# Diagonal and finest-level attention scores as channel sums of elementwise products, in the heads of a hybrid decoder step

## The chip, the cores and the metric

The kernel runs on one core of a Trainium2 chip. The metric is the device time of one execution in microseconds (us). Engines: TensorE (matmuls; PE in the profile, its weight loads PEld), VectorE (DVE), ScalarE (ACT), GpSimd (POOL) and SyncE (SP), which issues most of the transfers. They run side by side and meet at semaphores.

## The reference

One layer of a decoder for 256 prompt tokens and 8 sample tokens: a norm, a wide input projection, two gated recurrences (HGRN2 with 8 heads of 128 keys and 128 values, GLA with 4 heads of 128 keys and 256 values), their merge, an output projection, a squared-ReLU MLP and gated embeddings, all in float32. What matters here is the recurrence of the prompt, per head:

```python
b = jnp.cumsum(gi, axis=-2)
diff = b[..., :, None, :] - b[..., None, :, :]
decay = jnp.exp(jnp.where(causal, diff, -jnp.inf))
scores = jnp.einsum('bhtk,bhsk,bhtsk->bhts', qi, ki, decay)
o = jnp.einsum('bhts,bhsv->bhtv', scores, vi) + ...
```

The score of a token t with an earlier token s is a sum over 128 channels of q, k and a decay that depends on channel, t and s. With s = t the decay is 1 and the score is the sum of q times k over the channels.

## The kernel before

**The stream.** All weights come as tiles of 128 output rows, each in two slabs of 128 x 1024. For each slab SP loads `raw`, ScalarE rounds it to `whi` (L355, `round_slab`), VectorE takes the rest `wlo` (L360, `rest_slab`), and TensorE multiplies: three products of 264 columns for each of 8 blocks (L380 to L382). Rounded operands have the type fp32r; a sum of three such products stands in for a float32 product. Four slots (`RING`) hold slabs; SP loads a slot again when VectorE has taken its rest, ScalarE rounds into it again when TensorE has multiplied it.

**The heads.** After the projections come twelve heads (H = 0 to 7 HGRN, 8 to 11 GLA), each beside four weight tiles, that is eight slabs of TensorE. Each engine has its program for a head written out by hand: `slab(k)` calls, and between them the head's own work. TensorE's slab(k) is slab k of the head's tiles; ScalarE's and VectorE's slab(k) is the one that TensorE multiplies two slabs later, so their slab(6) to slab(9) belong to the next head's first slabs or the last of this one. Every engine does its list in order.

**A head's scores.** The prompt is taken as two blocks of 128 tokens, the second one in mirrored order. Level 0 pairs the two blocks; level l = 1 to 7 pairs the halves of cells of 2h tokens, h = 128 >> l, so the finest, level 7, has h = 1. For each level, decay factors for q and k are made in `lev` (VectorE subtracts, ScalarE takes the exponential in `decays`), and multiplied with q and k by VectorE in `level_operands` (L1540 to L1544). The q side stays in `lev[:, l, 0, :]`, the k side goes to `k_lev`. TensorE then does, in `scores`, two diagonal products of k_b and q_b (L766), seven products for levels 1 to 7 (L768) and one for level 0 (L770), each 128 x 128 x 128 in float32, that is unrounded, which the profile lists as two records. VectorE masks the level scores with `both` (L1581), the diagonal blocks and level 0 with `ident` (L1584), and adds the levels into `pairs` (L1592). Then `prob_v` (L787, L788) multiplies `pairs` with the values.

**The order around it.** TensorE in a head: slabs 0 to 4, `turn_v` (transposes of the values, L757), `scores`, `turn_kd` (transposes of kd, L778), slabs 5 and 6, `prob_v`, `state` (in HGRN heads), slab 7 with the norm's sums inside. `scores` waits for VectorE's level products, `turn_kd` for VectorE's kd (L1559) and for ScalarE's copy of the turned values, `v_tok` (L1096), which shares a bank with it. ScalarE: slabs 2 to 6, `turned` (the v_tok copy), slab 7, the copy of kd, the squares for the norm and, in HGRN heads, their rounding `sq_hi` (L1153), slab 8, logs and exponentials, slab 9, `decays` of the next head, `b_hi`. VectorE: slab 2, level products, slab 3, level products, kd, slabs 4 and 5, a tile's drain, slab 6, masks and adds, slab 7, the next head's level factors, `sq_lo` (L1603) in HGRN heads, slab 8, more factors, slab 9, the output. In HGRN heads the norm is already done with `ones_r` and two rounded operands, `sq_hi` and `sq_lo` (L801, L802). GpSimd copies `cum`, `q_b` and `k_b` of the next head (L1934 to L1939) and in GLA heads adds the two squares (L1944).

Of the kernel before, what the change touches and what calls it, by code (L numbers as in the profile page):

```python
# [28 lines left out]
P = 128  # L29
D_MODEL = 2048  # L30
KT = D_MODEL // P
NP_TOK = 256
# [69 lines left out]
def build(nc, t):  # L102
# [79 lines left out]
    with nc.sbuf_tensor("gate_w", [2 * RANK, GH * P], F32) as gate_w, nc.sbuf_tensor("rank_z", [2 * RANK, TOK], F32) as rank_z:  # L182
        pass
    S = sb("S", [P, 2, UNIT])
    n_states = [S[:, 0, :], S[:, 1, :], samp[:, 0:UNIT]]
# [5 lines left out]
    with nc.sbuf_tensor("o_first", [P, TOK], F32), nc.sbuf_tensor("sq_lo", [P, NP_TOK], F32R) as sq_lo:  # L191
# [57 lines left out]
    by_engine = {  # L249
        "act": ["v_tok_ready", "lev_exp", "kd_exp", "kd_tok_ready", "sq_ready", "sq_rounded",  # L250
                "ln_rs", "rs_ready", "o_hi_done", "s_out_ready", "sg_abs", "sg_exp", "sg_ln", "sg_sigma"],
        "dve": ["sq_parted", "lev_sub", "lev_ready", "kd_ready", "masked", "probs_ready", "sg_ls",
                "sg_ready", "o_scaled", "o_gated", "o_done"],
# [51 lines left out]
    def before(H):  # L305

        return H + 1

    def cells(ap, h, at, step, pitch):

        return bass.AP(ap.tensor, ap.offset + at, [list(ap.ap[0]), [step, 2], [pitch, 64 // h], [1, h]])
# [4 lines left out]
    def lefts(ap, h):  # L316
        return cells(ap, h, 0, P + h, 2 * h)

    def packed(ap, h):
# [144 lines left out]
    def _(sp):  # L464
# [17 lines left out]
        for k in range(RING, KT - 4):  # L482
            load_wide(sp, T_RANK, k, T_RANK)
            if k in (RING, RING + 3):
                load_x(4 + (k - RING) // 3)
        for dst, name in ((masks, "masks"), (ident, "ident"), (head_gain, "head_gain"),
                          (gate_b, "gate_b")):
            sp.dma_start(dst[:], t[name]).then_inc(const_landed, 16)
        for part in range(2):
            sp.dma_start(gate_w[part * RANK:(part + 1) * RANK, :], t["gate_w"]).then_inc(const_landed, 16)  # L490
# [181 lines left out]
    def _(pe):  # L672
# [27 lines left out]
        pe.wait_ge(tiles_drained, T_RANK + WIDE)  # L700
        pe.wait_ge(const_landed, 16 * 6)
        for h in range(GH):
# [58 lines left out]
        def scores(H, D):  # L761
            pe.wait_ge(h_sem["lev_ready"], now(H))
            pe.wait_ge(h_sem["ln_rs"], before(H))
            for B in range(2):
                at = slice(B * P, (B + 1) * P)
                pe.matmul(DG[:, 2 * B * P:(2 * B + 1) * P], k_b[:, at], q_b[:, at], start=True, stop=True)  # L766
            for l in range(1, LEVELS):
                pe.matmul(SC[(l - 1) // 4][:, (l - 1) % 4 * P:((l - 1) % 4 + 1) * P], k_lev[:, l - 1, :], lev[:, l, 0, :],  # L768
                          start=True, stop=True)
            pe.matmul(DG[:, P:2 * P], lev[:, 0, 1, :], lev[:, 0, 0, :], start=True, stop=True)\  # L770
              .then_inc(h_sem["scores_done"], 1)

# [8 lines left out]
        def prob_v(H, D):  # L781

            pe.wait_ge(h_sem["probs_ready"], now(H))
            pe.wait_ge(h_sem["o_scaled"], before(H))
            for d in range(D):
                v = slice(d * P, (d + 1) * P)
                pe.matmul(O[d][:, 0:2 * P], v_tok[:, 0, v], pairs[:, 0:2, :], start=True, stop=False, skip_group_check=True)  # L787
                mm = pe.matmul(O[d][:, P:2 * P], v_tok[:, 1, v], pairs[:, 2, :], start=False, stop=True, skip_group_check=True)  # L788
            mm.then_inc(h_sem["pv_done"], 1)
# [8 lines left out]
        def head_norm(H, D):  # L798
            if D == 1:
                pe.wait_ge(h_sem["sq_parted"], now(H))  # L800
                pe.matmul(DG[:, 0:NP_TOK], ones_r[:], sq_hi[:], start=True, stop=False)  # L801
                pe.matmul(DG[:, 0:NP_TOK], ones_r[:], sq_lo[:], start=False, stop=True).then_inc(h_sem["ss_done"], 1)  # L802
                return
            pe.wait_ge(h_sem["sq_added"], now(H - HH))
            pe.matmul(DG[:, 0:NP_TOK], ones[:], sq[:, 0, 0:NP_TOK], start=True, stop=True).then_inc(h_sem["ss_done"], 1)

        def head(H, D, first=False):
            T = 4 * H + T_HEADS

            def slab(k, midway=None, at=HT // 2):  # L810
                j, half = k // 2, k % 2
                par = (T_HEADS + j) % 2
# [124 lines left out]
    def _(act):  # L937
# [178 lines left out]
        def head(H, D, next_D, first=False):  # L1116
# [34 lines left out]
            if D == 1:  # L1151
                act.wait_ge(h_sem["sq_ready"], now(H))
                act.copy(sq_hi[:], sq[:, 0, 0:NP_TOK]).then_inc(h_sem["sq_rounded"], 1)  # L1153
            if first:
# [172 lines left out]
    def _(dve):  # L1327
# [158 lines left out]
        dve.wait_ge(gates_stored, GH)  # L1486
        dve.wait_ge(const_landed, 16 * 6)
        dve.wait_ge(masks_ready, 1)
# [26 lines left out]
        def head(H, D, more=True, opening=False):  # L1515
# [20 lines left out]
            def level_operands(l):  # L1536
# [5 lines left out]
                lq, lk = packed(lev[:, l, 0, :], h), packed(lev[:, l, 1, :], h)  # L1542
                dve.tensor_tensor(lq, lq, rights(q_b[:], h), ALU.mult)
                return dve.tensor_tensor(cells(k_lev[:, l - 1, :], h, 0, h, 2 * h), lk, lefts(k_b[:], h), ALU.mult)  # L1544

            def first_levels():

                dve.wait_ge(h_sem["kq_ready"], now(H))
                dve.wait_ge(h_sem["lev_exp"], now(H))
# [3 lines left out]
            def last_levels():  # L1553
# [30 lines left out]
            dve.tensor_tensor(pairs[:], DG[:, 0:3 * P].rearrange("s (b t) -> s b t", b=3),  # L1584
                              ident[:].rearrange("s (b t) -> s b t", b=3), ALU.mult).then_inc(h_sem["masked"], 1)
            for l in range(1, LEVELS):
                h = HALF[l]
                to = cells(pairs[:, 0, :], h, h, 2 * P - h, 2 * h)
                of = packed(probs[:, l - 1, :], h)

                dve.wait_ge(h_sem["masked"], (LEVELS + 1) * H + (l + 3))
# [9 lines left out]
            if D == 1:  # L1601
                dve.wait_ge(h_sem["sq_rounded"], now(H))
                dve.tensor_tensor(sq_lo[:], sq[:, 0, 0:NP_TOK], sq_hi[:].bitcast(F32), ALU.subtract).then_inc(h_sem["sq_parted"], 1)  # L1603
            slab(8)
# [266 lines left out]
    def _(pool):  # L1871
# [27 lines left out]

        pool.wait_ge(const_landed, 16 * 6)  # L1900

# [29 lines left out]
        def head(H, D):  # L1931
# [7 lines left out]
            pool.tensor_copy(k_b[:, 0:NP_TOK], k).then_inc(h_sem["kq_ready"], 1)  # L1939

        def add_halves(H):

# [5 lines left out]
        for i, (hg, gla) in enumerate(((hk, zk), (hk, zk))):  # L1948
# [4 lines left out]
            else:  # L1953
                pool.tensor_copy(to[:, 0:HH, :], hg[:, :, at])
                pool.tensor_copy(to[:, HH:HEADS, :], gla[:, :, at])
        pool.tensor_copy(by_head(s_cols[:, 3, :, :]), gates[:, :, at]).then_inc(cols_ready, 1)
        with pool.Fori(1, HH) as H:
            head(H, 1)
        with pool.Fori(HH, HH + 1) as H:
            head(H, 2)  # L1960
        with pool.Fori(HH, HEADS - 1) as H:
            head(H + 1, 2)
            add_halves(H)
        add_halves(HEADS - 1)
# [98 lines left out]
```

## Time and profile before

| | |
|---|---|
| median of three runs | 1628.49 us (1628.38 to 1629.86) |
| the profiled execution's own time | 1628.97 us |
| its span, first to last instruction | 1627.2 us |
| granted TensorE clock | 1.00 (2.4 GHz) |
| TensorE busy | 1620.3 us (100%) |
| VectorE, ScalarE, GpSimd busy | 1109.9, 842.2, 181.7 us |
| HBM read, written | 310.08 MB, 18.30 MB |

A busy matmul engine is listed with overlapping records: a matmul's row is longer than the distance to the next one's start, and it is the distance that the engine is held. The same holds, less so, for VectorE and ScalarE, whose next instruction starts before the row of the last one ends. The chain that ended last gives each step the time that it adds.

### The profile page before, as it was taken

Reading aid. Unit: us, or ns where it says so; the run is one execution under the profiler, and the core shown is the slowest. Engines: PE = TensorE matmul, PEld = TensorE weight load, DVE = VectorE, ACT = ScalarE, POOL = GpSimd, SP = SyncE. Lnnn points to the kernel's source line nnn. Section 1 sums busy time; section 2 is a strip of 40 time slices with the busy share of each in tenths; the row PEclk is TensorE's granted clock in tenths of the full one; section 3 lists DMA queues with packets and bytes.
Section 4 is the critical chain, followed back from the end, with each engine's and each line's share of the span. In section 5 each row is a group of like instructions: output and inputs, shape, how many; then the busy total and the mean of one; then the engine's idle time right before and its main releaser. Section 6 shows DMA issues by size and latency. Waiting matters only on the chain.

```text
span 1627.2 us, 35049 instructions
## 1 busy us (share of the span) xinstructions
PE 1620.3 (100%) x13332; PEld 1615.8 (99%) x13332; DVE 1109.9 (68%) x1917; ACT 842.2 (52%) x1192; POOL 181.7 (11%) x166
## 2 busy tenths in 40 slices
PE   9999999999999999999999999999999999999999
PEld 9999999999999999999999999999999999999999
DVE  7548767888888876655986665566555665555774
ACT  7575765666666665433654334443444334443452
POOL 3101000111111100055300000000000000035200
PEclk9999999999999999999999999999999999999999
DMA  9577895565555467755675865588557775555564
GB/s 274 161 230 225 267 270 174 164 191 162 192 166 181 155 206 229 270 181 185 173 214 186 247 207 180 188 259 243 174 181 242 245 222 185 181 197 181 167 192 144
DMA packets 151178, 329.17 MB, mean 202 GB/s; under 512 B 16944, under 2 KB 79536, under 8 KB 150608
## 3 DMA queue, kind: packets, MB, share of 16 engines
q1 hardware_dynamic: 143888, 326.00, 64.3%
q10 hardware_dynamic: 7232, 2.43, 0.6%
q8 instruction: 33, 0.54, 0.1%
q14 instruction: 25, 0.20, 0.0%
HBM read 310.08 MB, written 18.30 MB: 202 GB/s over the span
## 4 chain that ended last, share of the span: by engine, by line
PE 98%; DMA 1%; DVE 1%; ACT 0%; SPq 0%; issue 0%
PE bank L380 29%; PE bank L381 29%; PE bank L382 28%; PE bank L398 3%; PE bank L400 3%; PE bank L403 2%; PE bank L768 1%; DMA raw<-in_stream 1%; PE bank L795 0%; PE bank L787 0%; PE bank L766 0%; PE bank L788 0%; PE bank L757 0%; PE bank L732 0%; PE bank L770 0%; PE bank L778 0%
## 5 line engine op out<-in xcount | busy, mean ns | idle before, releaser
L355 ACT CAST whi<-raw 128x1024 fp32r<-128x1024 f32 x532 | 547.9, 1048 | 470.7 <-PE bank L382 388.5
L380 PE MATMUL bank<-a_hi,whi 128*128 128x264 f32 x2576 | 734.2, 285 | 0.1
L381 PE MATMUL bank<-a_hi,wlo 128*128 128x264 f32 x2576 | 729.7, 283 | 0.0
L382 PE MATMUL bank<-a_lo,whi 128*128 128x264 f32 x2576 | 729.4, 283 | 0.0
L360 DVE TENSOR_TENSOR wlo<-raw,whi 128x1024 fp32r<-128x1024 f32 x518 | 629.6, 1246 | 109.8 <-ACT whi L355 108.8
L380 PEld LDWEIGHTS bank<-a_hi,whi 128*128 128x128 f32 x2576 | 485.2, 188 | 0.8 <-issue 0.7
L381 PEld LDWEIGHTS bank<-a_hi,wlo 128*128 128x128 f32 x2576 | 485.5, 188 | 0.1
L382 PEld LDWEIGHTS bank<-a_lo,whi 128*128 128x128 f32 x2576 | 482.9, 187 | 0.0
L380 PE MATMUL bank<-b_hi,whi 128*128 128x264 f32 x1280 | 363.1, 284 | 0.0
L381 PE MATMUL bank<-b_hi,wlo 128*128 128x264 f32 x1280 | 362.6, 283 | 0.0
L382 PE MATMUL bank<-b_lo,whi 128*128 128x264 f32 x1280 | 362.4, 283 | 0.0
L381 PEld LDWEIGHTS bank<-b_hi,wlo 128*128 128x128 f32 x1280 | 241.2, 188 | 0.0
L380 PEld LDWEIGHTS bank<-b_hi,whi 128*128 128x128 f32 x1280 | 241.1, 188 | 0.0
L382 PEld LDWEIGHTS bank<-b_lo,whi 128*128 128x128 f32 x1280 | 239.9, 187 | 0.0
L1281 ACT ACTIVATE lev<-lev 128x264 f32<-128x264 f32 x64 | 27.2, 425 | 165.5 <-DVE lev L1777 165.5
L1690 DVE TENSOR_TENSOR room<-room,bank 128x264 f32<-128x264 f32 (+1 forms) x48 | 20.6, 429 | 106.9 <-PE bank L382 106.9
L1883 POOL TENSOR_TENSOR sq<-room 128x264 f32<-128x264 f32 x2 | 2.2, 1086 | 721.9 <-DVE room L1690 620.0
L398 PE MATMUL bank<-b_hi,whi 128*128 128x264 f32 x256 | 73.3, 286 | 0.3 <-DVE b_lo L1339 0.3
L403 PE MATMUL bank<-b_hi,wlo 128*128 128x264 f32 x256 | 72.8, 284 | 0.0
L400 PE MATMUL bank<-b_lo,whi 128*128 128x264 f32 x256 | 72.7, 284 | 0.0
L1783 DVE TENSOR_TENSOR a_lo<-lev,a_hi 128x264 f32 (+1 forms) x64 | 27.3, 432 | 63.8 <-ACT a_hi L1283 63.8
L1777 DVE SCALAR_TENSOR_TENSOR lev<-bank,r_bc 128x264 f32<-128x264 f32 x64 | 27.1, 432 | 52.6 <-PE bank L382 52.5
(222 smaller groups left out, 1497.7 us busy)
## 6 DMA issues: line engine op xcount, KB each, us to landing
raw<-in_stream SPq DMA_DIRECT2D x532, 512.0 KB, 4.7
m_spill<-stage SPq DMA_DIRECT2D x32, 132.0 KB, 3.7
lev<-m_spill SPq DMA_DIRECT2D x16, 264.0 KB, 2.8
room<-in_x SPq DMA_DIRECT2D x7, 528.0 KB, 7.8
S<-in_state_hgrn SPq DMA_DIRECT2D x6, 512.0 KB, 6.7
out_new_hgrn_sample<-S SPq DMA_DIRECT2D x6, 512.0 KB, 6.8
S<-in_state_gla SPq DMA_DIRECT2D x5, 512.0 KB, 6.7
out_new_gla_sample<-S SPq DMA_DIRECT2D x5, 512.0 KB, 7.5
```

Source lines behind the costliest of these rows:

```text
L355: act.copy(whi[:, s, :], raw[:, s, :]).then_inc(hi_ready, 1)
L360: dve.tensor_tensor(wlo[:, s, :], raw[:, s, :], whi[:, s, :].bitcast(F32), ALU.subtract).then_inc(lo_ready, 1)
L380: pe.matmul(out, whi[:, s, w], hi[:, k0 + k, :], start=start and k == 0, stop=False)
L381: pe.matmul(out, wlo[:, s, w], hi[:, k0 + k, :], start=False, stop=False)
L382: mm = pe.matmul(out, whi[:, s, w], lo[:, k0 + k, :], start=False, stop=stop and k == HT - 1)
L398: pe.matmul(out, whi[:, s, w], hi[:, k, :], start=k == 0, stop=False, skip_group_check=True)
L400: mm = pe.matmul(out, whi[:, s, w], lo[:, k, :], start=False, stop=rank and k == KT - 1, skip_group_check=True)
L403: return pe.matmul(out, wlo[:, s, w], hi[:, k, :], start=False, stop=k == KT - 1, skip_group_check=True)
L1281: act.activation(u, u, ACT.Square).then_inc(u_ready, 1)
L1690: ins = dve.tensor_tensor(out, out, MM[par][:, 0:TOK], ALU.add)
L1777: dve.scalar_tensor_tensor(out=u, in0=bank[:, 0:TOK], scalar=0.0, in1=r_bc[:], op0=ALU.max, op1=ALU.mult).then_inc(tiles_drained, 1)
L1783: dve.tensor_tensor(a_lo[:, T - T0, :], u, a_hi[:, T - T0, :].bitcast(F32), ALU.subtract).then_inc(a_lo_ready, 1)
```

## The change

In every head, the two diagonal products and the level 7 product leave TensorE. Their scores are needed only where s = t, or between the two tokens of a pair, so each is one number per token: a sum over the channels (partitions) of an elementwise product. GpSimd multiplies q_b and k_b into two thirds of a new buffer `dots` (`dots_of`), VectorE multiplies the two sides of level 7 into the other third. ScalarE rounds the 384 columns to `dots_hi`, VectorE takes the rest `dots_lo`, and TensorE multiplies `ones_r` with both into 384 columns of the bank DG (`sum_dots`), after `turn_kd`. VectorE then masks level 7 from DG in an instruction of its own. The order of the blocks in `pairs` and `ident` changes, for which `ident` is loaded in three parts. VectorE's slab(6) moves from before the masks to behind the adds. The semaphores `sq_rounded` and `sq_parted` become `parts_rounded` and `parts_ready`, counted twice in an HGRN head. GpSimd's first `dots_of` waits until the sample states are summed, since `dots` lies where they lay.

```diff
     def scores(H, D):
-        pe.wait_ge(h_sem["lev_ready"], now(H))
+        pe.wait_ge(h_sem["lev_ready"], first_now(H))
         pe.wait_ge(h_sem["ln_rs"], before(H))
-        for B in range(2):
-            at = slice(B * P, (B + 1) * P)
-            pe.matmul(DG[:, 2 * B * P:(2 * B + 1) * P], k_b[:, at], q_b[:, at], start=True, stop=True)
-        for l in range(1, LEVELS):
+        for l in range(1, LEVELS - 1):
             pe.matmul(SC[(l - 1) // 4][...], k_lev[:, l - 1, :], lev[:, l, 0, :],
                       start=True, stop=True)
-        pe.matmul(DG[:, P:2 * P], lev[:, 0, 1, :], lev[:, 0, 0, :], start=True, stop=True)\
-          .then_inc(h_sem["scores_done"], 1)
+        pe.matmul(DG[:, 3 * P:4 * P], lev[:, 0, 1, :], lev[:, 0, 0, :], start=True, stop=True)
+
+    def sum_dots(H, D):
+        pe.wait_ge(h_sem["parts_ready"], dots_now(H, D))
+        pe.matmul(DG[:, 0:3 * P], ones_r[:], dots_hi[:], start=True, stop=False)
+        pe.matmul(DG[:, 0:3 * P], ones_r[:], dots_lo[:], start=False, stop=True).then_inc(h_sem["scores_done"], 1)
...
         scores(H, D)
         turn_kd(H)
+        sum_dots(H, D)
         slab(5)
...
 # ScalarE, head
         slab(5)
+        act.wait_ge(h_sem["kq_ready"], second_now(H))
+        act.wait_ge(h_sem["lev_ready"], second_now(H))
+        act.copy(dots_hi[:], dots[:]).then_inc(h_sem["parts_rounded"], 1)
         slab(6)
         turned(H, D)
...
 # VectorE, level_operands
+            if l == LEVELS - 1:
+                return dve.tensor_tensor(lk, lk, lefts(k_b[:], h), ALU.mult)
 # VectorE, last_levels, behind the kd product
+            dve.wait_ge(h_sem["lev_ready"], first_now(H))
+            dve.tensor_tensor(dots[:, 0:P], lev[:, LEVELS - 1, 0, :], lev[:, LEVELS - 1, 1, :], ALU.mult).then_inc(h_sem["lev_ready"], 1)
 # VectorE, head
         slab(4)
+        dve.wait_ge(h_sem["parts_rounded"], dots_now(H, D))
+        dve.tensor_tensor(dots_lo[:], dots[:], dots_hi[:].bitcast(F32), ALU.subtract).then_inc(h_sem["parts_ready"], 1)
         slab(5)
         ...
-        slab(6)
         dve.wait_ge(h_sem["scores_done"], now(H))
         dve.wait_ge(h_sem["pv_done"], before(H))
-        for n, (first, last) in enumerate(((0, 4), (4, LEVELS - 1))):
+        for n, (first, last) in enumerate(((0, 4), (4, LEVELS - 2))):
             ...
-        dve.tensor_tensor(pairs[:], DG[:, 0:3 * P]..., ident[:]..., ALU.mult)
+        dve.tensor_tensor(probs[:, LEVELS - 2, :], DG[:, 0:P], both[:, LEVELS - 2, :], ALU.mult).then_inc(h_sem["masked"], 1)
+        dve.tensor_tensor(pairs[:], DG[:, P:4 * P]..., ident[:]..., ALU.mult)
         for l in range(1, LEVELS):
             ...
+        slab(6)
...
 # GpSimd
+    def dots_of(H):
+        pool.wait_ge(h_sem["kq_ready"], first_now(H))
+        pool.tensor_tensor(turned_blocks(dots), q_b[:, 0:NP_TOK]..., k_b[:, 0:NP_TOK]..., ALU.mult).then_inc(h_sem["kq_ready"], 1)
...
+    pool.wait_ge(units_summed, HEADS)
+    with pool.Fori(0, 1) as H:
+        dots_of(H)
     with pool.Fori(1, HH) as H:
         head(H, 1)
+        dots_of(H)
...
 # SyncE
-        for dst, name in ((masks, "masks"), (ident, "ident"), (head_gain, "head_gain"),
-                          (gate_b, "gate_b")):
+        for dst, name in ((masks, "masks"), (head_gain, "head_gain"), (gate_b, "gate_b")):
             sp.dma_start(dst[:], t[name]).then_inc(const_landed, 16)
+        for to, of in ((0, 0), (1, 2), (2, 1)):
+            sp.dma_start(ident[:, to * P:(to + 1) * P], t["ident"][:, of * P:(of + 1) * P]).then_inc(const_landed, 16)
```

## Rows read from the trace of the kernel before

**Rows 1.** The page's busy times and chain, and the heads' window (busy us, records).
```profile
PE 1620.3 (100%) x13332; PEld 1615.8 (99%) x13332; DVE 1109.9 (68%) x1917; ACT 842.2 (52%) x1192; POOL 181.7 (11%) x166
...
PE 98%; DMA 1%; DVE 1%; ACT 0%; SPq 0%; issue 0%
...
264.50:587.00 322.50, 322.39 (x2650) 320.21 (x2649) 272.62 (x708) 200.83 (x291) 44.58 (x46) 1.00 0.54 172
```

**Rows 2.** The chain in heads 1, 4, 8 and 9: start, us added, step, records.
```profile
295.56 0.69 PE bank L766 x4
...
377.88 1.56 PE bank L768 x14
...
486.48 0.45 PE bank L766 x4
...
515.18 0.56 PE bank L766 x4
```

**Rows 3.** Timeline of TensorE at head 4's norm: start, length, line, form.
```profile
388.79 0.28 PE L801 MATMUL bank<-sq_hi,ones_r 128*128 128x256 f32 x1
388.90 0.28 PE L802 MATMUL bank<-sq_lo,ones_r 128*128 128x256 f32 x1
```

**Rows 4.** Timeline of VectorE in head 4, idle time before in brackets.
```profile
376.43 0.28 DVE L1544 TENSOR_TENSOR k_lev<-lev,k_b 128x128 f32<-128x128 f32 x1
376.63 0.42 DVE L1559 TENSOR_TENSOR kd<-kd,k_b 128x256 f32<-128x256 f32 x1
376.97 2.35 DVE L360 TENSOR_TENSOR wlo<-raw,whi 128x1024 fp32r<-128x1024 f32 x2
379.24 0.42 DVE L1373 TENSOR_TENSOR stage<-bank,r_bc 128x264 f32<-128x264 f32 x1
...
382.36 2.25 DVE L1592 TENSOR_TENSOR pairs<-pairs,probs 128x128 f32<-128x128 f32 x7
...
387.61 0.42 DVE L1603 TENSOR_TENSOR sq_lo<-sq,sq_hi 128x256 fp32r<-128x256 f32 x1
...
393.50 1.23 DVE L360 TENSOR_TENSOR wlo<-raw,whi 128x1024 fp32r<-128x1024 f32 x1 [1.45 <-ACT whi L355]
```

**Rows 5.** Timeline of ScalarE in head 4.
```profile
377.25 1.05 ACT L355 CAST whi<-raw 128x1024 fp32r<-128x1024 f32 x1 [1.85 <-PE bank L382]
378.20 0.37 ACT L1096 COPY v_tok<-bank 128x256 f32<-128x256 f32 x1
...
386.78 0.41 ACT L1153 CAST sq_hi<-sq 128x256 fp32r<-128x256 f32 x1
```

**Rows 6.** Timeline of TensorE's weight loads in head 4.
```profile
379.39 0.25 PEld L778 LDWEIGHTS bank<-ident,kd 128*128 128x128 f32 x2
...
388.67 0.19 PEld L801 LDWEIGHTS bank<-sq_hi,ones_r 128*128 128x128 f32 x1
```

**Rows 7.** Timelines of VectorE (heads 8, 9), ScalarE and weight loads (head 9).
```profile
485.24 0.41 DVE L1559 TENSOR_TENSOR kd<-kd,k_b 128x256 f32<-128x256 f32 x1
...
514.89 0.42 DVE L1559 TENSOR_TENSOR kd<-kd,k_b 128x256 f32<-128x256 f32 x1
...
514.78 1.05 ACT L355 CAST whi<-raw 128x1024 fp32r<-128x1024 f32 x1 [1.85 <-PE bank L382]
515.73 0.58 ACT L1096 COPY v_tok<-bank 128x512 f32<-128x512 f32 x1
...
515.03 0.52 PEld L766 LDWEIGHTS bank<-q_b,k_b 128*128 128x128 f32 x4
...
517.25 0.25 PEld L778 LDWEIGHTS bank<-ident,kd 128*128 128x128 f32 x2
```

**Rows 8.** Timeline of GpSimd in heads 4 and 9.
```profile
377.21 2.16 POOL L1934 COPY cum<-totals 128x2 f32 x1 [23.02 <-DVE kd L1559]
...
525.64 0.91 POOL L1944 TENSOR_TENSOR sq<-sq 128x256 f32<-128x256 f32 x1 [5.99 <-ACT sq L1149]
```

**Rows 9.** Timeline of SP's queue in the opening, four slab loads behind the tables.
```profile
31.35 6.08 SPq L348 DMA_DIRECT2D raw<-in_stream x4
```

More of the change, by code:

```diff
@@ L183, in build @@
         pass
+    with nc.sbuf_tensor("dots", [P, 3 * P], F32) as dots, nc.sbuf_tensor("dots_hi", [P, 3 * P], F32R) as dots_hi, \
+         nc.sbuf_tensor("dots_lo", [P, 3 * P], F32R) as dots_lo:
+        pass
     S = sb("S", [P, 2, UNIT])
@@ L249, in build @@
     by_engine = {
-        "act": ["v_tok_ready", "lev_exp", "kd_exp", "kd_tok_ready", "sq_ready", "sq_rounded",
+        "act": ["v_tok_ready", "lev_exp", "kd_exp", "kd_tok_ready", "sq_ready", "parts_rounded",
                 "ln_rs", "rs_ready", "o_hi_done", "s_out_ready", "sg_abs", "sg_exp", "sg_ln", "sg_sigma"],
-        "dve": ["sq_parted", "lev_sub", "lev_ready", "kd_ready", "masked", "probs_ready", "sg_ls",
+        "dve": ["parts_ready", "lev_sub", "lev_ready", "kd_ready", "masked", "probs_ready", "sg_ls",
                 "sg_ready", "o_scaled", "o_gated", "o_done"],
@@ L307, in before, with dots_now, first_now, second_now @@
         return H + 1
+    def dots_now(H, D):
+        return 2 * H + 2 if D == 1 else H + (HH + 2)
+    def first_now(H):
+        return 2 * H + 2
+    def second_now(H):
+        return 2 * H + 3
     def cells(ap, h, at, step, pitch):
@@ L317, in lefts, with turned_blocks @@
         return cells(ap, h, 0, P + h, 2 * h)
+    def turned_blocks(dots):
+        ap = dots[:, 2 * P:3 * P]
+        return bass.AP(ap.tensor, ap.offset, [list(ap.ap[0]), [-P, 2], [1, P]])
     def packed(ap, h):
@@ L700, in _ @@
         pe.wait_ge(tiles_drained, T_RANK + WIDE)
-        pe.wait_ge(const_landed, 16 * 6)
+        pe.wait_ge(const_landed, 16 * 8)
         for h in range(GH):
@@ L786, in prob_v @@
                 v = slice(d * P, (d + 1) * P)
-                pe.matmul(O[d][:, 0:2 * P], v_tok[:, 0, v], pairs[:, 0:2, :], start=True, stop=False, skip_group_check=True)
-                mm = pe.matmul(O[d][:, P:2 * P], v_tok[:, 1, v], pairs[:, 2, :], start=False, stop=True, skip_group_check=True)
+                pe.matmul(O[d][:, 0:2 * P], v_tok[:, 0, v], pairs[:, 1:3, :], start=True, stop=False, skip_group_check=True)
+                mm = pe.matmul(O[d][:, P:2 * P], v_tok[:, 1, v], pairs[:, 0, :], start=False, stop=True, skip_group_check=True)
             mm.then_inc(h_sem["pv_done"], 1)
@@ L799, in head_norm @@
             if D == 1:
-                pe.wait_ge(h_sem["sq_parted"], now(H))
+                pe.wait_ge(h_sem["parts_ready"], second_now(H))
                 pe.matmul(DG[:, 0:NP_TOK], ones_r[:], sq_hi[:], start=True, stop=False)
@@ L1152, in head @@
                 act.wait_ge(h_sem["sq_ready"], now(H))
-                act.copy(sq_hi[:], sq[:, 0, 0:NP_TOK]).then_inc(h_sem["sq_rounded"], 1)
+                act.copy(sq_hi[:], sq[:, 0, 0:NP_TOK]).then_inc(h_sem["parts_rounded"], 1)
             if first:
@@ L1486, in _ @@
         dve.wait_ge(gates_stored, GH)
-        dve.wait_ge(const_landed, 16 * 6)
+        dve.wait_ge(const_landed, 16 * 8)
         dve.wait_ge(masks_ready, 1)
@@ L1543, in level_operands @@
                 dve.tensor_tensor(lq, lq, rights(q_b[:], h), ALU.mult)
+                if l == LEVELS - 1:
+                    return dve.tensor_tensor(lk, lk, lefts(k_b[:], h), ALU.mult)
                 return dve.tensor_tensor(cells(k_lev[:, l - 1, :], h, 0, h, 2 * h), lk, lefts(k_b[:], h), ALU.mult)
             def first_levels():
-                dve.wait_ge(h_sem["kq_ready"], now(H))
+                dve.wait_ge(h_sem["kq_ready"], first_now(H))
                 dve.wait_ge(h_sem["lev_exp"], now(H))
@@ L1576, in head @@
                 gate_tile(1)
-            slab(6)
             dve.wait_ge(h_sem["scores_done"], now(H))
             dve.wait_ge(h_sem["pv_done"], before(H))
-            for n, (first, last) in enumerate(((0, 4), (4, LEVELS - 1))):
+            for n, (first, last) in enumerate(((0, 4), (4, LEVELS - 2))):
                 dve.tensor_tensor(probs[:, first:last, :], SC[n][:, 0:(last - first) * P].rearrange("s (l t) -> s l t", t=P),
                                   both[:, first:last, :], ALU.mult).then_inc(h_sem["masked"], 1)
-            dve.tensor_tensor(pairs[:], DG[:, 0:3 * P].rearrange("s (b t) -> s b t", b=3),
+            dve.tensor_tensor(probs[:, LEVELS - 2, :], DG[:, 0:P], both[:, LEVELS - 2, :], ALU.mult).then_inc(h_sem["masked"], 1)
+            dve.tensor_tensor(pairs[:], DG[:, P:4 * P].rearrange("s (b t) -> s b t", b=3),
                               ident[:].rearrange("s (b t) -> s b t", b=3), ALU.mult).then_inc(h_sem["masked"], 1)
@@ L1587, in head @@
                 h = HALF[l]
-                to = cells(pairs[:, 0, :], h, h, 2 * P - h, 2 * h)
+                to = cells(pairs[:, 0, :], h, P + h, -(P + h), 2 * h)
                 of = packed(probs[:, l - 1, :], h)
-                dve.wait_ge(h_sem["masked"], (LEVELS + 1) * H + (l + 3))
+                dve.wait_ge(h_sem["masked"], (LEVELS + 2) * H + (l + 4))
                 last = dve.tensor_tensor(to, to, of, ALU.add)
                 last.then_inc(h_sem["probs_ready" if l == LEVELS - 1 else "masked"], 1)
+            slab(6)
             if opening:
@@ L1601, in head @@
             if D == 1:
-                dve.wait_ge(h_sem["sq_rounded"], now(H))
-                dve.tensor_tensor(sq_lo[:], sq[:, 0, 0:NP_TOK], sq_hi[:].bitcast(F32), ALU.subtract).then_inc(h_sem["sq_parted"], 1)
+                dve.wait_ge(h_sem["parts_rounded"], second_now(H))
+                dve.tensor_tensor(sq_lo[:], sq[:, 0, 0:NP_TOK], sq_hi[:].bitcast(F32), ALU.subtract).then_inc(h_sem["parts_ready"], 1)
             slab(8)
@@ L1898, in _ @@
         add_squares(0)
-        pool.wait_ge(const_landed, 16 * 6)
+        pool.wait_ge(const_landed, 16 * 8)
         def side_masks(l, side):
@@ L1939, in head @@
             pool.tensor_copy(k_b[:, 0:NP_TOK], k).then_inc(h_sem["kq_ready"], 1)
+        def dots_of(H):
+            pool.wait_ge(h_sem["kq_ready"], first_now(H))
+            pool.tensor_tensor(turned_blocks(dots), q_b[:, 0:NP_TOK].rearrange("c (b t) -> c b t", b=2),
+                               k_b[:, 0:NP_TOK].rearrange("c (b t) -> c b t", b=2), ALU.mult).then_inc(h_sem["kq_ready"], 1)
         def add_halves(H):
@@ L1956, in _ @@
         pool.tensor_copy(by_head(s_cols[:, 3, :, :]), gates[:, :, at]).then_inc(cols_ready, 1)
+        pool.wait_ge(units_summed, HEADS)
+        with pool.Fori(0, 1) as H:
+            dots_of(H)
         with pool.Fori(1, HH) as H:
             head(H, 1)
+            dots_of(H)
         with pool.Fori(HH, HH + 1) as H:
             head(H, 2)
+            dots_of(H)
         with pool.Fori(HH, HEADS - 1) as H:
             head(H + 1, 2)
+            dots_of(H + 1)
             add_halves(H)
```

## The prediction

> **What bounds the kernel now.** I read the page first: its busy row and the chain that ended last. TensorE is busy for the whole span, and 98% of the chain lies on it; most of that is the streamed weight slabs, which the change leaves alone [rows 1]. So an instruction taken off TensorE is worth its full length, unless TensorE then waits. I then cut out the twelve heads (264.5 to 587 us): TensorE has no gap to speak of, VectorE works 272.62 of 322.50 us, ScalarE 200.83 [rows 1]. Third came the chain inside a head, for prices [rows 2], and last the timelines of VectorE, ScalarE, TensorE's weight loads and GpSimd around one HGRN head (head 4) and one GLA head (head 9), to see how late each partner is [rows 4 to 8]. The reader should see that TensorE is the bound with very little to spare: in heads 1 and 9 the first score products take 0.69 and 0.56 us instead of 0.45, so there it already stands for VectorE's level factors, by 0.24 and 0.11 us [rows 2].
>
> **What leaves and what comes on TensorE.** Four records (two diagonal products) take 0.45 us, fourteen (seven level products) 1.56 us: 0.223 us a product [rows 2]. Three go, 0.67 us a head. Two products of rounded operands with 384 columns come. Such products with 256 columns start 0.11 to 0.12 us apart [rows 3]. No row has 384. Bounds: 0.12 us each if the weight load sets the pace; 0.67 each if they cost what three unrounded products do. I take the columns' share, 0.115 x 384/256 = 0.17, because both are rounded products with the same weights: 0.34 a head. Net -0.33 us a head, -4.0 us over twelve, if nobody waits.
>
> **The new wait on ScalarE.** The sums need their operand split: ScalarE rounds it, VectorE takes the rest. ScalarE's copy stands between slab(5) and slab(6) and waits for VectorE's product for the finest level, which VectorE makes after the product for kd. Behind it on ScalarE are slab(6) and the copy of v_tok, and TensorE's turn_kd waits for v_tok. In head 4 the kd product starts at 376.63 and the next instruction at 376.97, so the new product runs 376.97 to 377.25, 0.28 us like every 128-column one [rows 4]. ScalarE would start slab(6) at 377.25 [rows 5]; now its copy starts near 377.30 (a signal takes some 0.05 us: the last level product starts 0.20 before kd's [rows 4], so in head 9 it ends near 514.97, and the weights that wait for it load at 515.03 [rows 7]). Its cost: 0.41 us for 256 columns and 1.05 for 1024 [rows 5] make 0.52 for 384, about 0.43 until the next one starts. So slab(6) starts at 377.72 and v_tok is copied 0.95 us later, 378.67 to 379.04; TensorE hears of it at 379.09. It would be at turn_kd at 379.39 [rows 6] less 0.67 = 378.72. A wait of 0.37 us against a gain of 0.33.
>
> In head 9 VectorE is later against TensorE. Its kd product starts at 514.89, so the new product ends at 515.50; slab(6), which ran at 514.78, moves to 515.98, and v_tok, now 0.58 us long, is there at 517.56. TensorE would come at 517.25 - 0.67 = 516.58 [rows 7]. It waits 0.98 us: +0.65 us a head, in heads 9 to 11. Head 1 is late in the same way, with the short copy of v_tok (0.37 us): wait 0.77, +0.44. In head 8 the kd product starts 1.24 us before the chain comes to the scores [rows 2, 7], in head 4 0.80 before (377.88 - 0.45 - 376.63 [rows 2, 4]): there the same sum leaves a wait of 0.16 and -0.17. In head 0 the level factors are made a whole stage earlier: no wait, -0.33.
>
> **VectorE's extra work.** 0.20 us for the product (128-column instructions start 0.20 apart [rows 4]); for the rest of the split 0.34 for 256 columns plus 128 columns at the slope to 1024 (2.27 us for two [rows 4]), 0.47 in all; one mask instruction more, 0.07, what the 0.20 has over 128 columns at that slope: together 0.74 us a head. Bounds: 0.5, and 1.0 if every instruction counts to its end. What is late next is sq_lo of the HGRN norm: it ends at 388.03 [rows 4], and the norm's weights load at 388.67 [rows 6], so 0.59 us is to spare. Shifted by 0.74, against a TensorE that is 0.04 later itself, it makes TensorE wait 0.11. But the next head's factors hang on ScalarE's chain from prob_v, so they then lead by 0.11 more and the first wait shrinks by 0.11: the two waits together stay 0.37, and heads 2 to 7 give +0.04 each. The shift goes no further: VectorE later stands 1.45 us for ScalarE [rows 4].
>
> **What is hidden.** slab(6)'s rest moves behind the masks and their adds. Ahead of the masks 1.13 us goes (2.27/2) and 0.67 comes, so they start 0.46 sooner and prob_v does not wait. The slab is multiplied only in the next head. SP's load for its slot, with load_v queued behind it, goes out near 385.3, after the adds (382.36 + 2.25 - 0.46 + 1.13), for a rounding that follows slab(9), whose rest is taken at 393.50 [rows 4]; without this cover it would cost up to the 4 us or so by which it moves. The level tables, the pairs' new order and level 7's contiguous store keep their sizes: nothing. The two extra table loads stand before four slab loads that SP spreads over 6.08 us by its own waits [rows 9]; uncovered, under 1 us once. GpSimd's product of 256 columns, 0.91 us by its nearest instruction, comes after q_b and k_b in the head before the one that uses it [rows 8]; if it came late, ScalarE's copy would wait as it does for VectorE's.
>
> GpSimd's two-column copy took 2.16 us while VectorE ran two slab rests, and those rests kept their usual time [rows 4, 8]: GpSimd gave way. The Trainium skill (GPSIMD Engine Reference, Key points) says that GpSimd shares its SBUF interfaces with VectorE and contends with VectorE instructions that have two SBUF inputs, without saying who pays. By the row the sum below stands; if VectorE paid, it would be the third rival's.
>
> **The sum.** Head 0 -0.33; head 1 +0.44 and a norm wait of 0.1, +0.5; heads 2 to 7 +0.24; head 8 -0.17; heads 9 to 11 +1.95: +2.2 us. The profiled execution took 1628.97 us, 0.48 over the median of the runs, 1628.49; the heads' change adds to either: 1630.7. The unknown costs alone (0.12 to 0.67 for a sum, 0.5 to 1.0 on VectorE, 0.1 either way in each wait) make it 1629.2 to 1633, the price of 0.67 apart, which the rounded rows speak against.
>
> **The rivals.** First, the change does what its counts say: no wait, -4.0 us, 1624.5. For it: TensorE alone is the bound, and the other engines have idle time. Against it: ScalarE takes its instructions in order, and the wait sits right before slab(6). It needs the operand about 0.4 us earlier in HGRN heads and 1 us earlier in GLA heads. Second, the slower side: VectorE's added work reaches the level factors of every head, so all heads from 1 on wait like a GLA head: 11 x 0.65 - 0.33 = +6.8, 1635.3. Against it stands the 1.45 us for which VectorE waits for ScalarE [rows 4]; it decides as soon as more than that is added between prob_v and the next factors. Third, VectorE stands still while GpSimd multiplies: 0.91 us more before sq_lo. The norm's wait grows from 0.11 to about 0.72 and the first wait disappears: 0.3 more in each of heads 1 to 7, +4.3 in all, 1632.8. Against it is the copy above.
>
> **How the numbers follow.** Forecast 0.65, first rival 0.13, second 0.15, third 0.07. The prediction is the forecast's 1630.7. The range takes in the first rival at its low end and the third and the forecast's upper bound at the other, 1624.5 to 1634.0, and leaves out the second. A change of 0.2% (3.3 us) is about what a measurement of this kernel can tell from none. Faster by more: most of the first rival, 0.11. Slower by more (above 1631.75): the second and third rival and a quarter of the forecast, 0.36. Within: 0.53.
>
> **What would show it.** In the changed kernel's profile: four fewer matmul records a head (six go, two come); the two sums start 0.17 us apart; in the chain a step at turn_kd that is longer than 0.22, by about 0.3 us in HGRN and 1 us in GLA heads, with ScalarE's slab(6) 0.5 and 1.2 us after slab 4's end; the norm's wait in HGRN heads about 0.1; the heads' stretch about 2 us longer and the rest the same. The prediction is wrong if turn_kd finds v_tok ready in HGRN heads, if the level factors come late in heads 2 to 7, or if the sums cost other than 0.17.

## The result and the profile after

The changed kernel takes 1631.71 us (median of 21 runs, 1630.30 to 1633.12) against 1628.48 for the kernel before (21 runs): ratio 1.0020, 95% interval 1.0014 to 1.0026. That is +3.2 us where +2.2 was forecast: inside the range, on the slower side, and the interval lies wholly above 1. The profiled execution has a span of 1629.6 us.

The page of the changed kernel, busy time and chain, which answer to [rows 1]:

```profile
PE 1618.5 (99%) x13284; PEld 1612.7 (99%) x13284; DVE 1120.3 (69%) x1953; ACT 847.0 (52%) x1204; POOL 191.9 (12%) x178
...
PE 85%; ACT 5%; DVE 5%; issue 3%; DMA 1%; ACTq 0%; SPq 0%; DVEq 0%
```

48 records left TensorE (12 heads by four), and its busy time fell by 1.8 us; yet the chain, 98% on TensorE before, now lies on ScalarE and VectorE for a tenth. That tenth is not lost time, since TensorE works beside it and is still busy for 99% of the span; it says how long other engines now set the pace. TensorE does less and waits. The waits of TensorE in the changed kernel (tile, releaser and its line: us, times, longest) say where; this row has no counterpart in the heads of the kernel before:

```profile
PE bank L800 <- ACT v_tok L1119: 4.6, 10, 0.8
```

L800 is turn_kd, L1119 the copy of v_tok, as forecast. What comes before that copy is seen in the chain of the changed kernel through head 4 (start, us added, step; L809 is prob_v of head 3):

```profile
358.73 0.43 PE bank L809 x2
...
376.77 0.20 DVE lev L1571
376.97 0.11 DVE kd L1587
377.08 0.14 issue
377.22 0.30 DVE dots L1589
...
377.60 0.07 ACT dots_hi L1164
...
378.01 1.04 ACT whi L375
379.06 0.28 ACT v_tok L1119
379.33 0.14 issue
379.47 0.41 PE bank L800 x2
379.88 0.18 PE bank L792
```

Between the end of prob_v (359.39) and turn_kd (379.47) the chain isn't on TensorE at all: 20 of a head's 27.3 us run over ScalarE's and VectorE's work for the norm and the next head's levels, and end with the last level product, the kd product, the new product (dots L1589), ScalarE's rounding of it (dots_hi L1164), slab(6) (whi L375), the copy of v_tok and turn_kd. The chain does the same before turn_kd of heads 1 to 6 and 9 to 11. There this way round sets the pace, and what TensorE saves is spent waiting at turn_kd. Of the rounding only 0.07 us stands here, because the rest of the 0.41 us to slab(6)'s start is listed as issue and sequencer steps. ScalarE's timeline in heads 4 and 9 of the changed kernel has the same three instructions with their lengths, against [rows 5, 7]:

```profile
377.60 0.51 ACT L1164 CAST dots_hi<-dots 128x384 fp32r<-128x384 f32 x1 [1.88 <-DVE dots L1589]
378.01 1.04 ACT L375 CAST whi<-raw 128x1024 fp32r<-128x1024 f32 x1
378.96 0.36 ACT L1119 COPY v_tok<-bank 128x256 f32<-128x256 f32 x1
...
515.93 0.51 ACT L1164 CAST dots_hi<-dots 128x384 fp32r<-128x384 f32 x1 [2.67 <-DVE dots L1589]
516.35 1.04 ACT L375 CAST whi<-raw 128x1024 fp32r<-128x1024 f32 x1
517.29 0.58 ACT L1119 COPY v_tok<-bank 128x512 f32<-128x512 f32 x1
```

ScalarE has stood idle 1.88 and 2.67 us when the operand comes: the same 1.85 us that it stood before for its slab's bank [rows 5], and more. TensorE's weight loads in the two heads, against [rows 6, 7]:

```profile
378.82 0.30 PEld L788 LDWEIGHTS bank<-lev 128*128 128x128 f32 x2
...
379.44 0.20 PEld L800 LDWEIGHTS bank<-ident,kd 128*128 128x128 f32 x2 [0.31 <-issue]
379.61 0.19 PEld L792 LDWEIGHTS bank<-dots_hi,ones_r 128*128 128x128 f32 x1
379.72 0.19 PEld L793 LDWEIGHTS bank<-dots_lo,ones_r 128*128 128x128 f32 x1
379.90 0.19 PEld L400 LDWEIGHTS bank<-a_hi,whi 128*128 128x128 f32 x1
...
388.91 0.19 PEld L402 LDWEIGHTS bank<-a_lo,whi 128*128 128x128 f32 x1
389.08 0.19 PEld L823 LDWEIGHTS bank<-sq_hi,ones_r 128*128 128x128 f32 x1
...
516.69 0.30 PEld L788 LDWEIGHTS bank<-lev 128*128 128x128 f32 x2
...
517.99 0.20 PEld L800 LDWEIGHTS bank<-ident,kd 128*128 128x128 f32 x2 [0.99 <-issue]
```

Without a wait L800 starts 0.23 us after L788 (377.83 and 378.06 in the kernel **Both** below); here it starts 0.62 and 1.30 after it, so the waits are 0.39 and 1.07. Such differences of starts, for all heads, make the table below: a head's time from one turn_v weight load to the next, and the wait at turn_kd in it.

```
head                    0      1      2-7 (each)       8      9-11 (each)
before, us            30.11  27.45   27.21           28.70   28.81 to 28.85
after, us             30.63  28.00   27.13 to 27.37  28.50   29.50 to 29.53
change, measured      +0.52  +0.55   +0.49 in all    -0.20   +2.06 in all
change, forecast      -0.33  +0.50   +0.24 in all    -0.17   +1.95 in all
wait, measured         0.90   0.86   0.39 to 0.46*    0.17   1.07
wait, forecast         none   0.77   0.37             0.16   0.98
                                     * head 7: 0.20
```

The changes add up to +3.42 us. What follows the heads is the same (1036.83 and 1036.82 us from the first projection weights to the last weight load). The spans differ by only 2.4 because the profiled execution of before came to head 0 at 264.97 us and that of after at 263.93; three more profiles of the kernel before came there at 263.89, 263.96 and 264.48.

### The profile page after: what moved, and what is told of

It reads as the page before. It is cut to its first block, busy times and chain, and to the rows that moved or that the text cites. A ratio compares the mean times of both kernels' runs of the same rounds, so it can differ in the third digit from the quotient of the medians.

```text
span 1629.6 us, 35081 instructions
## 1 busy us (share of the span) xinstructions
PE 1618.5 (99%) x13284; PEld 1612.7 (99%) x13284; DVE 1120.3 (69%) x1953; ACT 847.0 (52%) x1204; POOL 191.9 (12%) x178
## 4 chain that ended last, share of the span: by engine, by line
PE 85%; ACT 5%; DVE 5%; issue 3%; DMA 1%; ACTq 0%; SPq 0%; DVEq 0%
PE bank L401 25%; PE bank L400 25%; PE bank L402 25%; PE bank L418 3%; PE bank L420 3%; PE bank L423 3%; ACT whi L375 3%; DVE wlo L380 1%; DMA raw<-in_stream 1%; DVE lev L1569 1%; DVE k_lev L1572 1%; ACT L1185 1%; PE bank L809 0%; ACT room L1185 0%; PE bank L800 0%
## 5 line engine op out<-in xcount | busy, mean ns | idle before, releaser
L375 ACT CAST whi<-raw 128x1024 fp32r<-128x1024 f32 x532 | 548.2, 1048 | 447.5 <-PE bank L402 378.7
L1816 DVE TENSOR_TENSOR a_lo<-lev,a_hi 128x264 f32 (+1 forms) x64 | 27.3, 432 | 63.0 <-ACT a_hi L1309 63.0
```

Of the source, the lines that this page charges most:

```text
L375: act.copy(whi[:, s, :], raw[:, s, :]).then_inc(hi_ready, 1)
L1816: dve.tensor_tensor(a_lo[:, T - T0, :], u, a_hi[:, T - T0, :].bitcast(F32), ALU.subtract).then_inc(a_lo_ready, 1)
```

## The experiments

My theory: the rounding's place on ScalarE, ahead of slab(6) and v_tok, together with an operand that VectorE makes last, delays v_tok. Rival A: VectorE's 0.74 us more work a head is the cost, wherever the rounding stands. Rival B: slab(6)'s move behind the masks costs something. Ratios are to the kernel before on the same chip.

**The changed kernel again**, beside the others.

> The changed kernel once more, for a second profile. Both theories give some 1631.7 us (+3.2). Open is head 0: in the first profile its slab roundings on ScalarE stood 2.56 us for a weight transfer and TensorE 0.90 us at turn_kd, where I had forecast no wait. If that comes of the change, head 0 waits some 0.9 us here too; if it is the transfer's chance, the wait is under 0.3.

1631.62 us (11 runs), before 1628.22 (27 runs), ratio 1.0020 [1.0011, 1.0029]. The waits of heads 1 to 11 came back to 0.05 us; head 0's was 1.27 instead of 0.90. So head 0 varies, and the rest does not.

**The rounding behind v_tok**, alone.

```
 # ScalarE, head
             slab(5)
+            slab(6)
+            turned(H, D)
             act.wait_ge(h_sem["kq_ready"], second_now(H))
             act.wait_ge(h_sem["lev_ready"], second_now(H))
             act.copy(dots_hi[:], dots[:])...
-            slab(6)
-            turned(H, D)
```

> Only the place of ScalarE's copy to dots_hi is changed: behind the copy of v_tok instead of before slab(6). Theory (the copy and what it waits for delay v_tok, and that alone is the loss): the wait at turn_kd goes to 0 in all heads; since the sums still follow turn_kd, it comes back at the sums, about 0.7 us in HGRN heads and 0.55 in GLA heads (1.07 before), and VectorE, which waits for the copy ahead of slab(5), is up to 0.8 later at the norm: 1632 to 1635. Rival (VectorE's added work is what TensorE waits for, wherever ScalarE copies): 1631.7, with the wait still at turn_kd.

1638.48 us (4 runs), ratio 1.0063 [1.0048, 1.0078]. The direction was right, the size not: 1635 was the most expected. TensorE's waits in this kernel, and GpSimd's timeline in its head 9:

```profile
PE bank L792 <- DVE dots_lo L1603: 5.1, 12, 0.5
PE bank L827 <- POOL sq L1983: 2.5, 2, 1.3
...
PE bank L823 <- DVE sq_lo L1636: 1.6, 7, 0.2
PE bank L800 <- ACT v_tok L1119: 0.6, 1, 0.6
```

```profile
532.77 2.74 POOL L1983 TENSOR_TENSOR sq<-sq 128x256 f32<-128x256 f32 x1 [6.00 <-ACT sq L1175]
```

The wait at turn_kd is gone from heads 1 to 11, as it had to be if the rounding's place makes it. But, counted by the starts of the loads as in the table (the list above counts from the end of the load before, which is less), the sums (L792) now wait 0.68 us in nearly every head for dots_lo, the HGRN norm (L823) 0.5, and the GLA norm (L827) up to 1.63, for an add of GpSimd that took 0.91 us before [rows 8] and takes 2.74 here (last section). One wait was replaced by three.

**The sums later, with the rounding still in front.** TensorE runs the sums inside slab(5), VectorE takes dots_lo behind its slab(5), and sq_lo goes ahead of the next head's first levels.

```
 # TensorE, head
             turn_kd(H)
-            sum_dots(H, D)
-            slab(5)
+            slab(5, midway=lambda: sum_dots(H, D), at=3 if D == 1 else HT // 2)
 # VectorE, head
             slab(4)
+            slab(5)
             (dots_lo)
-            slab(5)
...
+            (sq_lo)
             if more:
                 level_half(0)
-            (sq_lo)
```

> The sums move into slab(5) (after 3 of its 8 blocks in HGRN heads, 4 in GLA), VectorE takes the rest dots_lo behind slab(5) and sq_lo before the next level factors; ScalarE's copy stays ahead of slab(6). Theory: the waits at turn_kd stay, 0.4 in HGRN and 1.0 in GLA heads, so 1631 to 1632. Rival (VectorE's work): the later places on VectorE's list take the wait away, 1625 to 1627.

1631.92 us, ratio 1.0023 [1.0014, 1.0032], with 0.80 us of wait at turn_kd in head 0, 0.86 in head 1, 0.46 to 0.51 in heads 2 to 6, 1.07 in heads 9 to 11: the changed kernel's own. Where the sums stand is not what costs.

**Both**: the edit above and the rounding behind v_tok.

> As e3_copy_front, and ScalarE's copy behind the copy of v_tok. Theory: no wait is left at turn_kd, the sums or the norm; 12 x (0.67 - 0.36) = 3.7 us are saved: 1624.8, at most 1625.5. Rival (VectorE's work): VectorE does all that it does in the changed kernel, so 1630 or more.

1626.34 us (11 runs), ratio 0.9988 [0.9979, 0.9997]: 5.6 us below the run before, from which only the rounding's place differs, and 1.9 us below the kernel before. ScalarE and the weight loads in its head 4:

```profile
376.58 1.05 ACT L375 CAST whi<-raw 128x1024 fp32r<-128x1024 f32 x1 [1.85 <-PE bank L402]
377.54 0.36 ACT L1118 COPY v_tok<-bank 128x256 f32<-128x256 f32 x1
377.80 0.51 ACT L1165 CAST dots_hi<-dots 128x384 fp32r<-128x384 f32 x1
```

```profile
377.83 0.30 PEld L788 LDWEIGHTS bank<-lev 128*128 128x128 f32 x2
378.06 0.25 PEld L800 LDWEIGHTS bank<-ident,kd 128*128 128x128 f32 x2
378.28 0.19 PEld L400 LDWEIGHTS bank<-a_hi,whi 128*128 128x128 f32 x1
...
379.38 0.19 PEld L792 LDWEIGHTS bank<-dots_hi,ones_r 128*128 128x128 f32 x1
```

slab(6) waits for its bank again and not for VectorE, v_tok is there before L800, and the sums come 1.1 us later without a wait. Heads 2 to 7 take 26.91 to 26.98 us, 0.23 to 0.30 below before: nearly the 0.33 of the count. VectorE's list is the one of the run before, and its work that of the changed kernel, so rival A falls. The kernel misses the expected 1624.8 to 1625.5, most of all by head 0 (wait 0.90 at turn_kd, although the rounding now stands behind v_tok) and head 1 (0.42 at the sums).

**slab(6)'s rest back ahead of the masks** on VectorE, all else as changed.

```
 # VectorE, head
+            slab(6)
             dve.wait_ge(h_sem["scores_done"], now(H))
...
-            slab(6)
             if opening:
```

> The changed kernel with VectorE's slab(6) put back before the masks; the rest of the change stays. Theory (the move is hidden, the copy's place is the loss): the masks end 1.13 us later, at most 0.1 us short of prob_v, so 1631.7 with the same waits at turn_kd. Rival (the moved rest costs): 2 us or more faster than the changed kernel.

1631.48 us (10 runs), before 1628.27, ratio 1.0018 [1.0009, 1.0028], with the same waits: the move is hidden. Rival B falls.

**The operand earlier**, the rounding where the change put it: VectorE makes the finest level's factors first among the last four levels and the product after the next level, so that two levels and kd come behind it; sq_lo as in the kernel with the sums later, which gained nothing by it. A counter of an earlier stage carries the signal, and TensorE's scores count one signal a head again.

```
 # VectorE, last_levels
-                for l in range(LEVELS // 2, LEVELS):
+                level_operands(LEVELS - 1).then_inc(halves_summed, 1)
+                level_operands(LEVELS // 2)
+                dve.wait_ge(halves_summed, 2 * H + (2 * HEADS + 1))
+                (product for dots).then_inc(halves_summed, 1)
+                for l in range(LEVELS // 2 + 1, LEVELS - 1):
 # ScalarE, head
-            act.wait_ge(h_sem["lev_ready"], second_now(H))
+            act.wait_ge(halves_summed, 2 * H + (2 * HEADS + 2))
             act.copy(dots_hi[:], dots[:])...
```

> The changed kernel with ScalarE's copy in its place before slab(6), but VectorE makes the finest level and its product first among the last four levels, so the copy's operand is there some 1.3 us sooner; sq_lo goes ahead of the next level factors, as in e4_all. Theory (ScalarE's copy stands for the product, and slab(6) and v_tok behind it): the copy fits into ScalarE's idle time before slab(6), the waits at turn_kd fall from 0.4 in HGRN and 1.07 in GLA heads to under 0.1; heads 1 and 9 to 11 pay 0.2 for the product ahead of the last level factors: 1626 to 1628. Rival (the copy's own 0.43 us is what delays v_tok, whenever its operand comes): HGRN waits stay 0.4, 1630 or more.

1627.40 us (11 runs), ratio 0.9998 [0.9989, 1.0007]. No wait at turn_kd in heads 1 to 11, heads 2 to 7 take 26.90 us. So it is not the 0.41 us of the rounding itself that delays v_tok but what it waits for. Head 9 loses 1.64 us, again at the GLA norm behind GpSimd's add.

**Both cures together**: the kernel **Both** with this order on VectorE.

> Both cures together: copy behind v_tok and the sums half a slab later, and the finest level's product ahead of three of VectorE's last level products. My theory: head 1's wait of 0.42 us at the sums goes, the rest stays as with the first cure alone (1626.3), so 1625.5 to 1626.5, unless GpSimd's add of squares again falls into a stretch in which VectorE runs without a gap (up to 1.6 us in a GLA head), then up to 1628. The rival that VectorE's added work is what costs gives no gain over the kernel before. Head 0's wait should again be 2.7 us less the lead of its third load.

1626.77 us (10 runs), before 1628.42, ratio 0.9988 [0.9979, 0.9998]: no better than the first cure alone, and slower than the 1625.5 to 1626.5 expected. Head 1's wait at the sums fell from 0.42 to 0.20 us, but the wait at its level products rose from 0.25 to 0.43, and that of heads 9 to 11 from 0.11 to 0.31. GpSimd's add did not make TensorE wait. Head 0 waited 0.55 us, where 2.7 less its lead would have been 0.93 (next experiment).

**The kernel before, three profiles more**, for head 0.

> The kernel before once more, for a second profile of head 0, whose wait at turn_kd (0.8 to 1.3 us) stands in all five profiles of kernels with the change, and not in the one of before. If the late weight transfers at the start of the heads come of the change, this profile has them on time again. If they are the transfers' chance, they may be late here too; TensorE should stand for them little or not, since before it comes to turn_kd 0.67 us later and v_tok 0.43 earlier.

> The kernel before again, one look, for head 0. In nine profiles so far the third load of the burst at the heads' start lets ScalarE round its slab 3.97 and 2.75 us ahead of head 0's turn_v in the kernel before, and 1.45 to 2.49 us ahead in the changed kernel and its variants; in the latter TensorE's wait at turn_kd is 2.7 us less this lead. If the lead is chance alone, this run may as well fall below 2.5 us; and the kernel before should still show no wait at turn_kd down to a lead of about 1.7, since its spare was 0.71 us at a lead of 2.75. If the change itself delays these loads, the lead stays above 2.5.

> The same once more, a fourth profile of the kernel before: same expectations for the lead of head 0's third load (chance: anywhere from 1.4 to 4; the change's doing: above 2.5) and no wait at turn_kd.

1627.70, 1627.97 and 1628.52 us. At the heads' start SP sends a burst of slab loads, and ScalarE rounds each slab as it lands. ScalarE from the third load of the burst on, first in the last of these three profiles, then in the changed kernel:

```profile
262.06 1.05 ACT L355 CAST whi<-raw 128x1024 fp32r<-128x1024 f32 x1 [1.03 <-DMA raw<-in_stream]
263.79 2.10 ACT L355 CAST whi<-raw 128x1024 fp32r<-128x1024 f32 x2
265.79 0.37 ACT L1096 COPY v_tok<-bank 128x256 f32<-128x256 f32 x1
```

```profile
262.09 1.05 ACT L375 CAST whi<-raw 128x1024 fp32r<-128x1024 f32 x1 [0.83 <-DMA raw<-in_stream]
...
263.83 1.03 ACT L375 CAST whi<-raw 128x1024 fp32r<-128x1024 f32 x1
264.77 0.51 ACT L1164 CAST dots_hi<-dots 128x384 fp32r<-128x384 f32 x1
265.18 1.04 ACT L375 CAST whi<-raw 128x1024 fp32r<-128x1024 f32 x1
266.13 0.36 ACT L1119 COPY v_tok<-bank 128x256 f32<-128x256 f32 x1
```

Here dots_hi has no idle time before it: in head 0 the operand is there early, as forecast, and the rounding just adds its 0.41 us to a ScalarE that is late with its slabs (the chain goes back from here to one of the loads, 8.26 us from 253.81 on). Call the time from this third slab's rounding to head 0's turn_v its lead. The four profiles of before have leads of 3.97, 2.75, 3.58 and 2.42 us and none waits at turn_kd (in the last, v_tok ends at 266.16 and L778 loads at 266.93). With the rounding in front, leads of 1.84, 1.45, 2.02, 1.71 and 2.49 gave waits of 0.90, 1.27, 0.80, 1.01 and 0.25: 2.7 us less the lead, each time within 0.12. With the rounding behind v_tok it was 2.3 us less the lead in two kernels: 0.83 at 1.49 (the rounding moved alone) and 0.55 at 1.77 (both cures together). In the kernel **Both** the lead of 1.90 came with 0.90 all the same, because there slab(6)'s own load landed late and ScalarE stood 0.39 us for it. The kernel before would wait from a lead of about 1.7 down (2.42 less 0.77 of spare and a little for the signal; worked out, not run). So at the lead of 1.84 the change's own doing is 0.9 us of wait against 0.31 gained: 0.4 of it is the rounding (2.7 less 2.3), and 0.5 comes of a TensorE that reaches turn_kd 0.67 us sooner and finds v_tok no earlier. Where the loads are late, moving the rounding cures less than half of the wait. Why the eight profiles with the change have leads of 1.45 to 2.49 and the four without 2.42 to 3.97 stays open: they nearly part, which chance seldom does, but 2.42 lies below the 2.5 that was expected if the change delayed the loads, SP issues the same loads in the same order at like times, and I found no cause.

## Why the prediction was right

**TensorE's count.** Four records a head fewer, as forecast. The sums start 0.18 us apart, and the next load after 0.18 (379.72, 379.90): 0.36 a head where 0.34 was priced from the columns. Net gain 0.31 a head.

**The wait on ScalarE.** Step by step as worked out. Head 4 began 0.31 us later than before, so forecast times shift by that: rounding 377.61 (measured 377.60), slab(6) 378.03 (378.01), v_tok 378.98 (378.96), L800 379.40 (379.44). Head 9, shifted by 0.32: product's end 515.82 (515.83), slab(6) 516.30 (516.35), v_tok's end 517.88 (517.87). The waits of 0.39 and 1.07 stand against 0.37 and 0.98, and head 8's 0.17 against 0.16 (0.14 by the rows' own sum). Head 7's 0.20 against 0.37 is a miss: the forecast took head 4 for all of heads 2 to 7, but in the kernel before VectorE started head 7's kd product 0.51 us ahead of turn_v, against 0.31 in heads 3 to 6. That the time fell inside the range says little, since the range is 9.5 us wide; the waits head by head are what bears the forecast out. That this mechanism, and not the work on VectorE, costs the time is shown by the pair of kernels that differ in the rounding's place alone (1631.92 and 1626.34), and by the earlier operand (1627.40).

**VectorE's extra work.** sq_lo in head 4 is 0.69 us later against the head's start, where 0.74 was priced. VectorE in the changed kernel, against [rows 4]:

```profile
376.89 0.42 DVE L1587 TENSOR_TENSOR kd<-kd,k_b 128x256 f32<-128x256 f32 x1
377.22 0.28 DVE L1589 TENSOR_TENSOR dots<-lev 128x128 f32<-128x128 f32 x1
...
378.56 0.55 DVE L1603 TENSOR_TENSOR dots_lo<-dots,dots_hi 128x384 fp32r<-128x384 f32 x1
...
388.61 0.42 DVE L1636 TENSOR_TENSOR sq_lo<-sq,sq_hi 128x256 fp32r<-128x256 f32 x1
```

It ends at 389.03, and the norm's weights load at 389.08, 0.17 us after the load before them, where 0.12 stood in the kernel before: the forecast norm wait of 0.11 us came at half its size (0.05 to 0.08 in heads 1 to 7). The forecast had let the first wait shrink by the 0.11; it did not, and 0.39 came at turn_kd. How little spare there is, the kernel with only the rounding moved shows: its norm waits about 0.5 in HGRN heads 1 to 7.

**What is hidden.** slab(6)'s move, by its own experiment. GpSimd's product took 0.74 us and nothing waited for it. The third rival's collision didn't come: VectorE's lengths in the heads are those of before. But the row against it, in which GpSimd gave way, was no rule, and here the prediction had luck. In head 4 GpSimd's product ran from 381.38 to 382.12, beside VectorE's masks, which read a bank and one SBUF tile, and VectorE's first add of two SBUF tiles began at 382.21. In three of the kernels above GpSimd began first, and VectorE did stand still, 0.48 us in each of three GLA heads (last section). The rival's norm wait of 0.72 does not come out of its terms either: 0.11 and 0.91 make 1.02.

**The step that was off**: head 0, forecast at -0.33, measured at +0.52. "The level factors are made a whole stage earlier: no wait" holds for the operand; but the step looked at the operand alone and left out that ScalarE is itself late in head 0, behind the burst of slab loads. So v_tok came later by the rounding's 0.41 us, and TensorE, 0.67 us sooner, stood for it: of the wait of 0.90, 0.4 is the rounding and 0.5 the late slabs. This is 0.85 of the 1.2 us by which the heads' sum (+3.42) passes the forecast (+2.2); the rest is 0.25 in heads 2 to 7 (0.04 a head forecast, 0.08 measured) and 0.11 in heads 9 to 11. None of the rivals came.

## What to carry to other kernels

On an engine that works in order, ask of a new instruction not how long it lasts but what it waits for and what stands behind it: 0.5 us of rounding cost 0.4 to 1.1 us a head because its operand was made last, and moving it behind the two instructions that TensorE needs, with its consumers moved too, turned +3.2 us into -1.9. A wait that is removed frees the next one, so move the consumer and the neighbours that share its slack together (with the rounding alone moved, the kernel was 10 us slower than before). Once the chain runs over other engines for most of a head, as here before turn_kd, work taken off the busy engine can only turn into waiting until that way is shortened (read from the chain; no run took off more to show it). Where an engine lives off a burst of loads, look at its lateness there separately, in several profiles, because the steady rows say nothing of it.

## What the runs showed of the hardware

GpSimd's add of squares (128 x 256, two SBUF inputs) took 0.91 us before and 2.74 us in the kernel with only the rounding moved. VectorE's timeline there, while the add was pending (its record runs 532.77 to 535.51):

```profile
532.70 0.28 DVE L1473 TENSOR_TENSOR lev<-cum 128x128 f32<-128x128 f32 x1
...
533.51 0.29 DVE L1473 TENSOR_TENSOR lev<-cum 128x128 f32<-128x128 f32 x1
533.72 1.22 DVE L380 TENSOR_TENSOR wlo<-raw,whi 128x1024 fp32r<-128x1024 f32 x1
535.71 0.71 DVE L1641 SCALAR_TENSOR_TENSOR room<-room 128x528 f32<-128x528 f32 x1 [0.78 <-ACT room L1185]
```

VectorE runs back to back at its usual lengths until 534.94, and the add ends 0.57 us after that; TensorE, which waits for the add, loads L827 at 535.57, so its end is not the record's error. In head 9 of the kernel with the early operand it took 2.75 us and ended 0.58 after VectorE's last. In the kernel before, VectorE ended a subtraction at 525.95 and then paused:

```profile
526.52 1.22 DVE L360 TENSOR_TENSOR wlo<-raw,whi 128x1024 fp32r<-128x1024 f32 x1 [0.57 <-ACT whi L355]
```

The add, 525.64 to 526.55, ended 0.60 us after VectorE's last instruction. So here it was GpSimd that waited, for the whole run of VectorE's instructions, and an add that fell into a run without a pause lasted three times as long.

The other way round occurs too. In the three kernels with the sums inside slab(5), the add starts some 0.13 us before VectorE's first subtraction for the next levels; head 9 of the kernel **Both**, GpSimd and VectorE:

```profile
523.35 0.74 POOL L1982 TENSOR_TENSOR sq<-sq 128x256 f32<-128x256 f32 x1 [4.79 <-ACT sq L1174]
523.48 0.76 DVE L1469 TENSOR_TENSOR lev<-cum 128x128 f32<-128x128 f32 x1
```

The add takes 0.74 us, the shortest of all these runs, and the subtraction 0.76 in place of 0.28. So neither engine always gives way; in these rows the one that came second waited. The Trainium skill (SBUF — State Buffer, SBUF: two separate sides) says that VectorE instructions with two SBUF inputs and GpSimd share a port pair under an exclusive lock that whoever starts first holds for its whole instruction. The trace agrees: the side that came second got nothing done until the other ended, as far as the lengths tell. That GpSimd did not get in between the VectorE instructions, which start 0.20 us apart, is what these rows add.
